# Expert values gathered by token and summed in four column groups, tile by tile

## What is computed

```python
s = jnp.einsum('thpd,hpnd->thpn', q, subkeys)          # 8 heads, 2 halves, 128 keys
half_s, half_i = lax.top_k(s, 16)
cand = half_s[:, :, 0, :, None] + half_s[:, :, 1, None, :]
best_s, best_i = lax.top_k(cand.reshape(n_tok, 8, 256), 16)
experts = i1 * 128 + i2                                 # 128 experts for each token
gates = jax.nn.softmax(best_s, axis=-1)
act = gelu(einsum('td,tkd->tk', x, take(u_tab, experts))) * gates
out = einsum('tk,tkd->td', act, take(v_tab, experts))
```

## Time and profile before

| what | value |
|---|---|
| median of 3 runs (lowest, highest) | 3099.57 us (3098.86, 3105.06) |
| span of the profiled execution | 3171.6 us |
| PE busy | 2560.4 us, 81% |
| DVE busy | 2033.0 us, 64% |
| POOL busy | 1459.4 us, 46% |
| ACT busy | 883.5 us, 28% |
| moved by DMA | 1071.04 MB, mean 338 GB/s |
| of that, gathers of POOL's queue | 805.39 MB |

### The profile page before, as it was taken

The page is one execution under the profiler, slowest core; times in us unless marked ns, Lnnn a source line. Parts: engine busy times, 40 slices in busy tenths (PEclk is TensorE's granted clock), DMA queues, the critical chain, the costliest instruction groups (busy, mean ns, idle before and its releaser), DMA issues. The chain is left out here.

```text
span 3171.6 us, 30406 instructions
## 1 busy us (share of the span) xinstructions
PE 2560.4 (81%) x8952; PEld 1459.0 (46%) x8952; DVE 2033.0 (64%) x4699; ACT 883.5 (28%) x2652; POOL 1459.4 (46%) x1284
## 2 busy tenths in 40 slices
PE   7899886978786769979997778888898777766666
PEld 3576633757553223356653224456666433232222
DVE  4522578876787884245448834677666888865665
ACT  1121123552222232144222211255412233222221
POOL 0000265554447775435456772555435344434442
PEclk9899998999988889988998899889899899989888
DMA  8757597979879999989999996988788799999996
GB/s 328 286 196 232 187 393 289 336 276 347 298 289 351 356 355 414 414 336 339 392 381 384 338 367 204 362 323 310 273 331 321 266 425 423 420 402 421 425 426 291
DMA packets 259362, 1071.04 MB, mean 338 GB/s; under 512 B 29440, under 2 KB 32256, under 8 KB 225664
## 3 DMA queue, kind: packets, MB, share of 16 engines
q0 software_dynamic: 184320, 805.39, 65.6%
q1 hardware_dynamic: 71712, 253.16, 21.3%
q10 hardware_dynamic: 3168, 10.55, 0.9%
HBM read 1065.67 MB, written 3.31 MB: 337 GB/s over the span
## 5 line engine op out<-in xcount | busy, mean ns | idle before, releaser
L782 PE MATMUL psum<-ring,wdiag 128*128 128x512 f32 x1396 | 727.3, 668 | 230.7 <-ACT wdiag L1074 153.8
L1752 POOL DMA_INDIRECT ring<-in_peer_u,experts x372 | 451.5, 1214 | 912.8 <-DVE dots L1309 442.2
L782 PEld LDWEIGHTS psum<-ring,wdiag 128*128 128x128 f32 x1396 | 285.6, 214 | 630.1 <-issue 577.0
L782 PE MATMUL psum<-work,wdiag 128*128 128x512 f32 x808 | 422.7, 668 | 168.3 <-ACT wdiag L1074 129.0
L1752 POOL DMA_INDIRECT ring<-in_peer_v,experts x410 | 448.2, 1093 | 230.4 <-issue 115.1
L1309 DVE CUSTOM_DVE_ANT_0 work<-work 128x1024 f32<-128x1024 f32 x270 | 326.6, 1226 | 127.6 <-DMA work<-in_peer_uv,experts 79.2
L1309 DVE CUSTOM_DVE_ANT_0 ring<-ring,work 128x1024 f32<-128x1024 f32 x242 | 292.7, 1225 | 139.0 <-DMA ring<-in_peer_uv,experts 90.3
L1309 DVE CUSTOM_DVE_ANT_0 ring<-ring,h2a 128x1024 f32<-128x1024 f32 x256 | 305.2, 1221 | 109.5 <-DMA ring<-in_peer_u,experts 103.9
L782 PEld LDWEIGHTS psum<-work,wdiag 128*128 128x128 f32 x808 | 161.7, 211 | 413.1 <-issue 395.8
L1065 ACT ACTIVATE acts<-dots 128x2 f32<-128x2 f32 x384 | 77.8, 203 | 930.1 <-DVE dots L1309 851.4
L872 PE MATMUL psum<-work,wring 128*128 128x256 f32 (+1 forms) x1760 | 329.7, 347 | 6.2 <-issue 5.7
(11 more groups left out here) (203 smaller groups left out, 2980.5 us busy)
## 6 DMA issues: line engine op xcount, KB each, us to landing
wring<-in_wpack SPq DMA_DIRECT2D x370, 512.0 KB
ring<-in_wpack SPq DMA_DIRECT2D x98, 512.0 KB, 6.3
ring<-in_peer_v,experts POOLq DMA_INDIRECT x410
ring<-in_peer_u,experts POOLq DMA_INDIRECT x372
work<-in_rows ACTq DMA_DIRECT2D x4, 1024.0 KB
wring<-in_wpack SPq DMA_DIRECT2D x16, 160.0 KB
work<-in_peer_u,experts POOLq DMA_INDIRECT x140
work<-in_peer_uv,experts POOLq DMA_INDIRECT x130
```

What stands on the lines that cost most here:

```text
L782: last = nc.tensor.matmul(psum[:, 6 + q, :], wdiag[:, SUM_NO[e] % SMALL, :], row("v", e)[:, 512 * q:512 * (q + 1)], start=(e % KSEL == 0), ...
L1752: pool.indirect_dma_start(dst, None, table, index).then_inc(got[ROW_SLOT[key]], 16)
```

## The change

The rows of u are fetched and multiplied as before, but separately for all tiles. The rows of v are fetched the other way round: one ask fetches the 128 experts of one token, one expert to each partition. For that the expert numbers are turned once per tile: `xi` (a transpose on PE, evacuated by DVE into `v_experts`). The weights are turned as well: when all 128 dots are through Gelu (four calls of 32) and multiplied by the gates on DVE (`gm`), PE transposes the weights of the tile (`xw`) and ACT copies them into `z`, a tensor of zeros in which each token has one column between 31 columns of zeros (`zf`, eight fills of 16 tokens). A product of a window of 32 columns of `z` with the v rows of a token adds that token's sum to its own partition of a group of 32 and zeros to the others. A step `v` takes four tokens, one in each of the partition groups 0 to 31, 32 to 63, 64 to 95 and 96 to 127: eight products of 512 columns.

The order is new too. For each tile there are first all 128 dots, then the turn (`gm`, `xw`, `zf`), then all 32 steps of sums, then the finish. The rows are asked for in this order (`ASKS`), so that no v row is asked for before the last u row of its tile, and no u row of a tile before the last v row of the tile before. All v rows go through PE: the sums on DVE, the diagonal matrices on ACT, `fsum` and the joined table are gone. Beside stage 1 (and 3) the dots of tile 0 (3) take the first half and its sums the second; the dots of tile 1 (4) lie in the `topk` of stage 1 (3); beside stage 2 lie the sums of tile 1, the dots of tile 2 and its sums; at the end come the sums and finish of tile 4, the dots of tile 5, its sums and finish. Cells stay 11 and 21.

```diff
+def dots_of(n):
+    out = []
+    for k in range(KSEL):
+        out.append(("u", n, k))
+        if k % GROUP == GELU_LAG and k > GROUP:
+            out.append(("gm", n, k // GROUP - 1))
+    return out
+def turn(n):
+    return [("gm", n, HEAD_GROUPS - 1), ("xw", n), ("zf", n, 0), ("zf", n, 1)]
...
+        n = TILE_NO[(STAGES[m][0], 0)]
+        first = PLACE[("topk", 0, 0, 1, 3)] if m == 0 else PLACE[("begin", 3)] + 1
+        chosen = PLACE[("topk", m + 1, 0, 0, 0)]
+        half = part(first, chosen, 0.5)
+        dots = dots_of(n)
+        if m:
+            set_(finish_items(n - 1), PLACE[("begin", 3)])
+        lay(dots[8 * (m > 0):], first, half)
+        set_(turn(n), half + 2)
+        last = PLACE[("topk", m + 1, 0, 2, 0)]
+        lay(sums_list(n, True), half + 3, last)
+        if m == 0:
+            one, two = dots_of(1), dots_of(2)
+            lay(one, PLACE[("topk", 1, 0, 1, 2)], PLACE[("begin", 2)])
...
+            early, middle = part(b, done, 0.3), part(b, done, 0.6)
+            set_(turn(1), b)
+            lay(flat(sums_of(1)) + finish_items(1), b + 1, early)
+            lay(two, early, middle)
+            set_(turn(2), middle + 2)
+            lay(flat(sums_of(2)), middle + 3, done)
+            set_(dots_of(3)[:8], done + 1)
+        else:
+            lay(dots_of(4), PLACE[("topk", 3, 0, 1, 2)], end)
+            five = dots_of(5)
+            set_(turn(4) + flat(sums_of(4)) + finish_items(4) + five, end)
+            set_(turn(5) + flat(sums_of(5)) + finish_items(5), end)
...
+                def add_rows(n, i):
+                    if i == 0 and n:
+                        pe.wait_ge(sums_free, n)
+                    if i % FILL == 0:
+                        pe.wait_ge(z_filled, FILLS * n + i // FILL + 1)
+                    for c in range(4):
+                        key = ("v", n, 4 * i + c)
+                        pe.wait_ge(got[ROW_CELL[key]], 16 * ROW_USE[key])
+                    for q in range(2):
+                        for c in range(4):
+                            o = 4 * i + c
+                            at = QUARTER * (o % Z_TOKENS + 1) - 1 - i
+                            last = nc.tensor.matmul(psum[QUARTER * c:QUARTER * (c + 1), 6 + q, :], z[:, at:at + QUARTER],
+                                                    row(("v", n, o))[:, 512 * q:512 * (q + 1)], start=(i == 0), stop=(i == V_STEPS - 1))
+                    last.then_inc(rows_added, 1)
```

More of the change, by code:

```diff
@@ L275, in stage_items @@
     out += [("ps", m, i, q) for i in range(T) for q in range(4)]
-    out += [("topk", m, i, g, n) for i in range(T) for g in range(HEAD_GROUPS) for n in range(TOPK_PIECES)]
-    return out
+    for i in range(T):
+        for g in range(HEAD_GROUPS):
+            for n in range(TOPK_PIECES):
+                out.append(("topk", m, i, g, n))
+                if i and (g, n) == (0, 4):
+                    out.append(("xi", m, i - 1))
+    return out + [("xi", m, T - 1)]
 def work():
@@ new lines, in sums_of, with finish_items, beside @@
+def sums_of(n):
+    out = []
+    for i in range(V_STEPS):
+        b = i // FILL
+        fill = [("zf", n, b + 1)] if i % FILL == 0 and 0 < b < FILLS - 1 else []
+        out.append(fill + [("v", n, i)])
+    return out
+def finish_items(n):
+    return [("fg", n, q) for q in range(2)] + [("fin", n)] + [("fl", n, q) for q in range(4)]
+def beside(dots, sums, lag):
+    out = dots[:lag]
+    rest = dots[lag:]
+    per = -(-len(rest) // len(sums))
+    for n, x in enumerate(sums):
+        out += x + rest[per * n:per * (n + 1)]
+    return out
@@ new lines, in flat, with part, lay, set_ @@
+def flat(groups):
+    return [x for g in groups for x in g]
+def part(first, last, share):
+    total, done = sum(cost(x) for x in WORK[first:last]), 0.0
+    for n in range(first, last):
+        done += cost(WORK[n])
+        if done >= total * share:
+            return n
+    return last
+def schedule():
+    at = {}
+    end = len(WORK)
+    def lay(items, first, last):
+        for x, place in zip(items, deal(first, last, items)):
+            at.setdefault(place, []).append(x)
+    def set_(items, place):
+        at.setdefault(place, []).extend(items)
+    for m in CONTEXT:
+        n = TILE_NO[(STAGES[m][0], 0)]
[12 more added lines that the diff above has]
+            lay(one, PLACE[("topk", 1, 0, 1, 2)], PLACE[("begin", 2)])
+            b = PLACE[("begin", 2)]
+            done = PLACE[("topk", 2, 0, 2, 0)]
+            early, middle = part(b, done, 0.3), part(b, done, 0.6)
[10 more added lines that the diff above has]
+            set_(turn(5) + flat(sums_of(5)) + finish_items(5), end)
+    return at
@@ L394, with row_cells @@
-VECTOR_SUM = vector_sums()
-def by_vector(e):
-    return VECTOR_SUM[e]
-SUM_NO, _sums = [], {True: 0, False: 0}
-for _e in range(ALL_EXPERTS):
-    SUM_NO.append(_sums[by_vector(_e)])
-    _sums[by_vector(_e)] += 1
-def sums_before(e, vector):
-    return sum(by_vector(i) == vector for i in range(e))
+ASKS = []
+for _x in PROGRAM:
+    if _x[0] == "u":
+        ASKS.append(_x)
+    elif _x[0] == "v":
+        ASKS += [("v", _x[1], 4 * _x[2] + _c) for _c in range(4)]
+def row_cells():
+    cell, use, before, uses, last, when = {}, {}, {}, [0] * CELLS, [None] * CELLS, [-1] * CELLS
+    for at, key in enumerate(ASKS):
+        c = min(range(RINGS if key[1] in TIGHT else CELLS), key=lambda i: when[i])
+        uses[c] += 1
+        cell[key], use[key], before[key] = c, uses[c], last[c]
+        last[c], when[c] = key, at
+    return cell, use, before
@@ L444, in evacuator @@
     return FIXED_BY[kind]
[L447 removed]
+NO_PSUM = ("begin", "macc", "norms", "outs", "ln1_rows", "ln1", "topk", "u", "gm", "zf", "v", "fin")
 ITEMS = [x for x in PROGRAM if x[0] not in NO_PSUM]
```

354 lines of the change are left out of this document (127 added, 227 removed).

## The result

| | before | after |
|---|---|---|
| median | 3099.51 us (4 runs) | 3294.54 us (4 runs, 3286.10 to 3312.77) |
| ratio | 1 | 1.0627, interval 1.0593 to 1.0661 |

What follows compares the result with a forecast made beforehand. The prediction took the latent stages as bound by the PE, DVE and ACT chain, the end by bytes. Stage 1 -50, middle +20, stage 3 -40, end +110 gave +40: span 3212, times 0.977, 3139 us; range 3010 to 3275.

Steps and rivals of the forecast that it cites:

- the factor 0.977: Whole kernel: the median is 0.977 of the profiled span, turning 3212 us into 3139 us.
- Stage 1, PE's term: Stage 1 (400 to 916 us): L782's 100 us on PE go, 55 come back, so PE saves 45 us.
- Stage 1, DVE's term: Stage 1: DVE's 91 us of adds go, of which 15 us, about a sixth, count as gain.
- The turn: Stage 1, between dots and sums: PE waits at `xw` for DVE's last dot and `gm`, 8 to 10 us.
- Stage 3: 1905 to 2475 us: PE saves 20 us, DVE's removed adds give 28, less 8 for the turn: 40 us less.
- The middle: 916 to 1905 us: 286 + 660 + 63 = 1009 us against 989, 20 us more.
- The end: From 2475 us: `topk`, then dots and sums in phases, 807 us against 697, 110 more; at least 70 more.
- The locked asks: Rival, tile 5's starved dots: rows come each 2.29 us, 51 us more; span 3267, 3193 us. Chance 0.14.
- The rhythm of 1.7 us: End, tile 5's dots after the first 42: asks held by dots give 1.7 us a row, 86 rows 146 us.
- Column groups: Sums on PE: four column groups run at once, 1.72 us a step of four tokens, 55 us a tile.
- the rival built on that rule: Sums on PE: products overlap, weight loads don't; 1.4 to 3.0 us more a step, 3227 to 3328 us. Chance 0.07.
- The three rivals on the slower side: Asks locked at the worst (3193 us, chance 0.14), serial column groups (3760, 0.11), weight loads not overlapping (3227 to 3328, 0.07).

Runs made afterwards that it cites:

- short dots: The changed kernel with each dot over 64 of its 1024 columns: 3026.39 us, ratio 0.9734 to the kernel before.
- the single-input form: The kernel before with separate asks for tiles 4 and 5 and dots as plain sums of the u row: 3291.10 us, ratio 1.0382.

## Why the prediction was wrong

Three steps failed: the 45 us that PE was to save in stage 1, where nothing was saved; the missing term for DVE's load in the half of the stage that now holds all dots, 39 us by the run that spreads them; and the factor 0.977, 73 us, which belongs to the chip and not to the profiler.

The profiled span is 77 us above the forecast 3212: 81 from stage 1 and 23 from stage 3, less 17 in the middle and 10 at the end. Another 73 us are the factor 0.977, and the rest is the distance of this profile to the median.

- **The scale.** "The median is 0.977 of the span" took the gap between the first profile and the timed runs for a property of profiling. It was a slower chip, and the same factor can't be applied to a kernel with other transfers: before gains 60 us in its middle on a faster chip, the changed kernel 69 at its end and 5 in its middle.
- **Stage 1, PE's term: the step that failed first.** "PE saves 45 us" took all of L782 in the window of the earlier trace rows. Half of it lay before the stage's own work, in the `topk` of stage 0, where PE had slack. L782 alone (PE, PEld busy) in the trace of 3171.6 us, then the kernel after on the faster chip in its stage:

```profile
400.00:500.00 100.00, 47.84 (x98) 17.96 (x98) 0.94 0.99 385
500.00:916.00 416.00, 52.04 (x91) 19.45 (x90) 0.93 0.84 313
```
```profile
529.00:945.00 416.00, 56.56 (x448) 12.32 (x448) 0.91 0.82 288
```

  From 500 us on PE had 52 us of sums and now has 57, all of them behind the last dot. There was nothing to save.
- **Stage 1, DVE's term.** "I take 15 us" for the adds that go. They went (29 us of 500 to 640), but as many dots came into the first half in their place: the dots alone (DVE busy) took 40 us of 500 to 640 before and take 72 now.

```profile
500.00:640.00 140.00, 40.34 (x68) 0.91 0.84 304
```
```profile
500.00:640.00 140.00, 71.82 (x122) 0.75 0.81 299
```

  The diff said that the dots take half of the stage. The step from there to DVE's load in that half, 27 more dots in these 140 us, was not made, and the forecast has no term for it. With the dots over three quarters of the stage it ended 39 us earlier, more than the 31 to 35 us that the stage lost. These 39 us and the 45 of PE's term are about the 81 by which stage 1 missed; how far they overlap was not measured.
- **The turn.** 8 to 10 us were put down for PE's wait at `xw`. In the stages 1 and 3 of the changed kernel PE stood there 0.0 and 1.3 us; the sums began 6 to 9 us behind it. The wait that did come is at the other transpose, `xi`, which was counted at nothing: PE's product at L1046 stands behind DVE's L1531, 58 us before stage 1 (452 to 509), and 628 us in all six places together. In stage 0's `topk` it is not what stage 1 waits for: PE's products of that stage begin at 529 us on the faster chip, behind DVE's L1441, where those of the kernel before began at 513. What the other five waits cost was not measured.

```profile
509.20 0.45 PE L1046 MATMUL psum<-consts,work 128*128 128x128 f32 x1 [57.56 <-DVE experts L1531]
529.24 1.09 PE L915 MATMUL psum<-work,wring 128*128 128x64 f32 x4 [19.60 <-DVEq L1441]
```

- **Stage 3.** 20 us of PE's time were right (76 to 57), the 28 us for DVE's adds gave nothing: 17 us won on the faster chip, 9 on the slower.
- **The middle.** 1009 us forecast, 994 to 1000 measured. The length is right (`topk` with dots 293 against 286, the rest 701 against 723), against a kernel before of 988 to 991. On the faster chip before needs only 928, and the +20 become +68.
- **The end.** On the faster chip term by term: `topk` with dots 295 (forecast 285), sums 149 (144), finish 10 (10), dots of tile 5 175 (194), turn and sums 163 (162), finish 13 (12). On the slower chip, the sort to which the trace belonged: 307, 175, 17, 177, 185 and 13, hence 874 instead of 807. The term that was mis-sized there is the gather: 1.27 us a row came from one window of 10 us. The same trace had 331 to 374 GB/s at a DMA share of 0.90 to 0.96 wherever separate rows ran long; at 367 GB/s, as the slower chip had in the sums of tile 5, an ask is 1.43 us, and 363 asks cost 58 us more, of the 67 us that are missing. That the forecast 807 fits the faster chip's 805 is luck: the trace was of the other sort.
- **The locked asks.** The rhythm of 1.7 us came only in part: in the dots of tile 5 the asks are 1.43 and 1.49 us apart on average on faster chips and 1.60 on the slower one, 1.25 to 1.28 in the median; on the faster chips 35 and 51 of the 128 took over 1 us. The ask and the dot find a common beat for long runs: an ask that starts 1.1 us into a dot is not held up and the next is again due at the same place. POOL and DVE beside each other, tile 5:

```profile
3041.18 0.94 POOL L1752 DMA_INDIRECT ring<-in_peer_u,experts  x1 [0.30 <-issue]
3042.43 0.94 POOL L1752 DMA_INDIRECT ring<-in_peer_u,experts  x1 [0.30 <-issue]
3043.67 1.61 POOL L1752 DMA_INDIRECT ring<-in_peer_u,experts  x1 [0.31 <-issue]
```
```profile
3040.08 1.23 DVE L1300 CUSTOM_DVE_ANT_0 ring<-ring,work 128x1024 f32<-128x1024 f32 x1
3041.32 1.23 DVE L1300 CUSTOM_DVE_ANT_0 ring<-ring,work 128x1024 f32<-128x1024 f32 x1
...
3043.24 1.23 DVE L1300 CUSTOM_DVE_ANT_0 ring<-ring,work 128x1024 f32<-128x1024 f32 x1 [0.68 <-DMA ring<-in_peer_u,experts]
```

  The third ask met a dot 0.43 us old and ended 2.04 us after that dot's start (3043.67 + 1.61 - 3043.24), as in the earlier trace rows. The mechanism was right, its frequency was taken too high: 194 us for the dots of tile 5 with 41 for the lock, where 168 and 175 were measured on faster chips and 149 with short dots, so 19 to 26 for the lock (30 on the slower chip). The Trainium skill (SBUF — State Buffer, Who interferes with whom) has a DVE instruction with two SBUF inputs contend with a GpSimd instruction that reads SBUF; the trace agrees, since with one input all asks of tile 5 took 0.94 us.
- **Column groups.** Right: four records at once, each four 0.43 us behind the last, 1.72 us a step, and 57 us a tile in stage 1 against 55 forecast. The Trainium skill (TensorE: Matmul & The Clock Gate, Part 3) lets weight loads overlap only with products of another row group; here all four groups use the same rows, and loads of 32 columns still lay beside running products:

```profile
2852.09 0.15 PEld L782 LDWEIGHTS psum<-work,z 128*32 128x32 f32 x6
2852.51 0.11 PEld L782 LDWEIGHTS psum<-ring,z 128*32 128x32 f32 x1 [0.27 <-issue]
```

  The measurement decides: the rival built on that rule did not come.

The three rivals on the slower side named other mechanisms, and none of these came at its price. None said that in the latent stages DVE would become the bound first and PE second. That DVE paces the kernel wherever dots stand alone with `topk` was in the forecast (285 us), but only as time for the rows, not as what two halves of a stage do to each other.

What stays open: why the chips (or the groups of runs) differ, what makes the pauses on the slower ones, and why separate rows cost 76 us in the kernel before on a faster chip, where they come at up to 420 GB/s in the changed one. There the asks took 1.05 us on average and came 1.36 us apart over the last 300 us, against 1.25 with short dots. Dots holding them up would be 512 times 0.11, 56 us; but the single-input form was not run on such a chip, on the slower one it changed nothing, and the DMA share there is 1.00 at 385 GB/s (2900 to 3150 us), which speaks for the transfers themselves. Of the 68 us that the middle lost on the faster chip no run shows the parts.

## What to carry to other kernels

Before a term says "this engine is freed", cut the window where the bound changes, and count the removed work only in the part where its engine was the limit. Work that is put into phases loads each engine by its own phase: divide the busy time by the phase, not by the stage, since an engine at 75% of a stage may be asked for more than 100% of half of it. Keep beside each instruction that loads a full engine some transfer that doesn't need this engine, and take the price of a gather from the longest stretch at full queue, with every chip that the runs have seen.

## What the runs showed of the hardware

- The same gathers average differently from one chip (or group of runs) to another: separate 4 KB rows at the end of the changed kernel 367 GB/s on a slower chip, with pauses of 5 us, and 419 on a faster one without; yet 419 GB/s were reached on the slower chip too, for 130 us in the dots of tile 5 with one input. Joined rows of 8 KB came at 419 to 425 on both sorts.
- Four products in column groups of 32, with their weight loads, start within 0.05 us of each other, and eight take 1.92 to 1.95 us at the full granted clock and 3.64 to 3.66 at half of it, whether issued group by group or half by half.
- An indirect ask that starts 0.1 to 1.1 us into a two-input DVE instruction ends 2.04 us after that instruction's start. One that starts 1.1 us into it takes its 0.94 us, and both settle into a beat of 1.25 us.
